# Norm weights kept in PSUM, token tiles finished in turn, channel tiles turned in two goes: the passage between the two mixers of a 1-core kernel

## What is computed

```python
# end of the first mixer
mix = jnp.concatenate([y_att, y_ssm], axis=-1)
out = jnp.einsum('bse,ed->bsd', mix, w_out[layer])
x = layer_norm(alpha * x + out, ln_g[layer], ln_b[layer])
# beginning of the second
mod = cond @ ada_w[i] + ada_b[i]
shift, scale, gate = jnp.split(mod, 3, axis=-1)
hdn = rms_norm_2(x, norm_g[i]) * (1.0 + scale[:, None, :]) + shift[:, None, :]
proj = h @ w_in          # h is hdn; w_in is 1024 x (4096 + 2048 + 32)
```

## Time and profile before

| | |
|---|---|
| median of 3 runs | 1055.65 us (1055.5 to 1058.39) |
| profiled execution | 1055.48 us, span of the trace 1053.5 us |
| PE matmul busy | 1022.1 us, 97% |
| DVE busy | 653.0 us, 62% |
| ACT busy | 434.2 us, 41% |
| POOL busy | 225.3 us, 21% |
| granted PE clock, mean | 0.997 of full speed |

### The profile page before, as it was taken

One profiled execution on the slowest core, in us unless ns is written; L12 is line 12 of the kernel. 1 busy time (PEld: TensorE's weight loads), 2 busy tenths in 40 slices (PEclk: granted clock), 3 DMA queues, 4 the chain that ended last, 5 costly groups with the idle time before them and its releaser, 6 DMA issues. The chain is left out here.

```text
span 1053.5 us, 14031 instructions
## 1 busy us (share of the span) xinstructions
PE 1022.1 (97%) x5374; PEld 830.3 (79%) x5374; DVE 653.0 (62%) x1078; ACT 434.2 (41%) x866; POOL 225.3 (21%) x169
## 2 busy tenths in 40 slices
PE   8999999999999999999899999999999998999997
PEld 5888888888766687788678788878888877888886
DVE  4254656622247778757746757785596777976726
ACT  4222333332358854332523333356423458134432
POOL 0010000000001352103100001100106873046792
PEclk9999999999999999999999999999999999999999
DMA  8277643233313242241423437435332213213502
GB/s 314 80 235 258 217 135 115 80 120 110 131 52 101 97 181 84 83 154 41 170 81 120 161 131 271 158 120 181 115 125 77 65 60 101 72 59 111 180 2 80
DMA packets 60818, 132.35 MB, mean 126 GB/s; under 512 B 6096, under 2 KB 6480, under 8 KB 60624
## 3 DMA queue, kind: packets, MB, share of 16 engines
q1 hardware_dynamic: 58304, 118.67, 33.1%
q0 software_dynamic: 2304, 12.58, 3.3%
q10 hardware_dynamic: 144, 0.20, 0.1%
HBM read 117.22 MB, written 14.22 MB: 125 GB/s over the span
## 5 line engine op out<-in xcount | busy, mean ns | idle before, releaser
L290 DVE TENSOR_TENSOR w_lo<-raw,w_hi 128x2048 fp32r<-128x2048 f32 x57 | 134.2, 2355 | 214.5 <-ACT w_hi L286 198.5
L286 ACT ACTIVATE w_hi<-raw 128x2048 fp32r<-128x2048 f32 x51 | 97.4, 1912 | 200.3 <-PE projections_ps L126 156.9
L124 PE MATMUL projections_ps<-projections_x_hi,w_hi 128*128 128x512 f32 x208 | 81.1, 390 | 0.4 <-ACTq L646 0.4
L126 PE MATMUL projections_ps<-projections_x_hi,w_lo 128*128 128x512 f32 x208 | 80.9, 389 | 0.0
L125 PE MATMUL projections_ps<-projections_x_lo,w_hi 128*128 128x512 f32 x208 | 80.9, 389 | 0.0
L124 PE MATMUL projections_ps<-w_hi,projections_x_hi 128*128 128x512 f32 x192 | 74.9, 390 | 0.0
L126 PE MATMUL projections_ps<-w_hi,projections_x_lo 128*128 128x512 f32 x192 | 74.7, 389 | 0.0
L125 PE MATMUL projections_ps<-w_lo,projections_x_hi 128*128 128x512 f32 x192 | 74.7, 389 | 0.0
L247 DVE SCALAR_TENSOR_TENSOR resid<-resid,mixer_cw 128x512 f32<-128x512 f32 x96 | 64.9, 745 | 0.0
L747 POOL TENSOR_TENSOR tok<-tok,attention_recip 128x512 f32<-128x512 f32 x8 | 8.3, 1041 | 229.9 <-DVE attention_recip L835 229.9
L124 PE MATMUL projections_ps<-w_hi,output_m_hi 128*128 128x512 f32 x128 | 51.2, 400 | 3.0 <-DVE resid L1560 1.9
(11 more groups left out here) (369 smaller groups left out, 2511.7 us busy)
## 6 DMA issues: line engine op xcount, KB each, us to landing
raw<-in_w_in SPq DMA_DIRECT2D x26, 1024.0 KB, 5.0
raw<-in_gdn_w_in SPq DMA_DIRECT2D x24, 1024.0 KB, 5.1
tok<-in_ada_w POOLq DMA_DIRECT2D x16, 768.0 KB, 6.4
raw<-in_w_out SPq DMA_DIRECT2D x8, 1024.0 KB, 5.0
qkv_kept<-mixer_ring SPq DMA_DIRECT2D x8, 1024.0 KB, 4.2
mixer_st<-qkv_kept SPq DMA_DIRECT2D x32, 256.0 KB, 2.9
raw<-in_gdn_w_out SPq DMA_DIRECT2D x7, 1024.0 KB, 5.2
resid<-in_att_bias SPq DMA_DIRECT2D x16, 256.0 KB, 2.7
```

Source lines behind the costliest of these rows:

```text
L124: nc.tensor.matmul(out, w_hi, x_hi, start=first, stop=False, skip_group_check=True)
L126: return nc.tensor.matmul(out, w_lo, x_hi, start=False, stop=last, skip_group_check=True)
L286: self.nc.scalar.activation(self.hi[s][:], self.raw[s][:], ACT.Copy).then_inc(self.hi_ready, 1)
L290: engine.tensor_tensor(self.lo[s][:], self.raw[s][:], self.hi[s][:], ALU.subtract)\
```

## The change

Five edits, all at the passage.

1. ACT copies `row_g` into two PSUM banks (`gains`), and DVE's L1625 takes its factor from there.
2. DVE finishes one token tile before it begins the next: `before_factor` and `after_factor` become one loop. POOL does `layer_factor(t)` and then `last_factor(t)`. ACT writes the scaled tile t right after its square, not after the square of the next.
3. Of the rest of the second mixer's first weight unit, DVE makes kk = 0, 1 at the end of the first block, and kk = 2, 3 in the second.
4. PE turns the token tiles 0 to 2 of the channel tiles e = 0..3 before it waits for `xn_ok`, and then token tile 3 of each.
5. In the first unit of the first block PE goes over kk outside and over e inside. The turns of the channel tiles 4 to 7 still stand ahead of each kk at e = 0. The second unit is as before.

```diff
+        early_hi, g_kept = sem("early_hi"), sem("g_kept")
+        gains = ps[:, 6:8, :].rearrange("p b c -> p (b c)")
...
@@ ACT, end of the first mixer
+                act.wait_ge(rows_in, 64)
+                act.wait_ge(added, GROUPS + TT)
+                nc.scalar.activation(gains, row_g[:], ACT.Copy).then_inc(g_kept, 1)
                 for t in range(TT):
                     if t == 2:
                         act.wait_ge(ahead[0], 48)
                         act.wait_ge(w.units_used, 9)
-                        nc.scalar.activation(w.hi[0][:], raw[0][:], ACT.Copy)
+                        nc.scalar.activation(w.hi[0][:], raw[0][:], ACT.Copy).then_inc(early_hi, 1)
...
-                    if t:
-                        act.wait_ge(factor_ok, ROW_FACTOR[t - 1])
-                        nc.scalar.activation(tok[:, t - 1, 0:D_MODEL], resid[:, t - 1, :], ACT.Copy, scale=row_f[:, t - 1:t])
+                    if t < TT - 1:
+                        act.wait_ge(factor_ok, 4 + 2 * t)
+                        nc.scalar.activation(tok[:, t, 0:D_MODEL], resid[:, t, :], ACT.Copy, scale=row_f[:, t:t + 1])
@@ POOL
-            layer_factor(0)
             for t in range(TT):
-                if t + 1 < TT:
-                    layer_factor(t + 1)
+                layer_factor(t)
                 last_factor(t)
@@ DVE, end of the first mixer
-                def before_factor(t):
+                dve.wait_ge(rows_in, 64)
+                dve.wait_ge(g_kept, 1)
+                for t in range(TT):
...
-                                                           scalar=mean_var[:, t, 0:1], in1=row_g[:],
+                                                           scalar=mean_var[:, t, 0:1], in1=gains,
                                                            op0=ALU.subtract, op1=ALU.mult))
-                    return own.n
-
-                def after_factor(t, step):
-                    dve.wait_ge(factor_ok, LAYER_FACTOR[t])
-                    own.wait(step)
+                    dve.wait_ge(factor_ok, 3 + 2 * t)
+                    own.wait()
                     nc.vector.scalar_tensor_tensor(out=resid[:, t, :], in0=resid[:, t, :], scalar=ln_f[:, t:t + 1],
                                                    in1=row_b[:], op0=ALU.mult, op1=ALU.add).then_inc(normed, 1)
-
-                dve.wait_ge(rows_in, 64)
-                step = before_factor(0)
-                for t in range(TT):
-                    next_step = before_factor(t + 1) if t + 1 < TT else None
-                    after_factor(t, step)
-                    step = next_step
                 dve.wait_ge(mod_sum, 1)
...
+                dve.wait_ge(early_hi, 1)
+                nc.vector.tensor_tensor(w.lo[0][:, 0:2, :], raw[0][:, 0:2, :], w.hi[0][:, 0:2, :], ALU.subtract)
@@ PE, beginning of the second mixer
-            def turn_x(e):
+            def turn_x(e, tiles=range(TT)):
                 if e >= 4:
                     pe.wait_ge(h_ok, e - 3)
-                for t in range(TT):
+                for t in tiles:
                     tr = nc.tensor.transpose(ps[:, 4 + e % 4, t * P:(t + 1) * P], xn[:, t, e * P:(e + 1) * P], ident)
-                tr.then_inc(h_turned, 1)
+                return tr
+            for e in range(4):
+                turn_x(e, range(TT - 1))
             pe.wait_ge(xn_ok, 1)
             for e in range(4):
-                turn_x(e)
+                turn_x(e, (TT - 1,)).then_inc(h_turned, 1)
...
+            KK_FIRST = [(kk, e) for kk in range(HALF) for e in range(4)]
+            E_FIRST = [(kk, e) for e in range(4) for kk in range(HALF)]
             pe.wait_ge(banks_free, 1)
             for s in range(2):
                 w.wait_unit(pe, s, 0)
-                for e in range(4):
-                    for kk in range(HALF):
+                for kk, e in (KK_FIRST, E_FIRST)[s]:
...
-                                turn_x(4 + kk)
+                            turn_x(4 + kk).then_inc(h_turned, 1)
@@ DVE, beginning of the second mixer
-            w.rest(nc.vector, dve, 0, 0)
+            nc.vector.tensor_tensor(w.lo[0][:, 2:HALF, :], raw[0][:, 2:HALF, :], w.hi[0][:, 2:HALF, :], ALU.subtract)\
+                .then_inc(w.lo_ready, 1)
```

More of the change, by code:

```diff
@@ L1159, in scan_and_output @@
         mod_sum = sem("mod_sum")
-        LAYER_FACTOR, ROW_FACTOR = (3, 4, 6, 8), (5, 7, 9, 10)
+        early_hi, g_kept = sem("early_hi"), sem("g_kept")
+        gains = ps[:, 6:8, :].rearrange("p b c -> p (b c)")
         def head_row(values):
@@ L1621, in before_factor @@
                     own.wait()
-                    nc.vector.bn_aggr(mean_var[:, t, :], stats[:, t, :, :].rearrange("p a b -> p (a b)"))\
-                        .then_inc(var_ok, 1)
+                    nc.vector.bn_aggr(mean_var[:, t, :], stats[:, t, :, :].rearrange("p a b -> p (a b)")).then_inc(var_ok, 1)
                     dve.wait_ge(var_ok, t + 1)
                     own.did(nc.vector.scalar_tensor_tensor(out=resid[:, t, :], in0=resid[:, t, :],
-                                                           scalar=mean_var[:, t, 0:1], in1=row_g[:],
+                                                           scalar=mean_var[:, t, 0:1], in1=gains,
                                                            op0=ALU.subtract, op1=ALU.mult))
-                    return own.n
-                def after_factor(t, step):
-                    dve.wait_ge(factor_ok, LAYER_FACTOR[t])
-                    own.wait(step)
+                    dve.wait_ge(factor_ok, 3 + 2 * t)
+                    own.wait()
                     nc.vector.scalar_tensor_tensor(out=resid[:, t, :], in0=resid[:, t, :], scalar=ln_f[:, t:t + 1],
                                                    in1=row_b[:], op0=ALU.mult, op1=ALU.add).then_inc(normed, 1)
-                dve.wait_ge(rows_in, 64)
-                step = before_factor(0)
-                for t in range(TT):
-                    next_step = before_factor(t + 1) if t + 1 < TT else None
-                    after_factor(t, step)
-                    step = next_step
                 dve.wait_ge(mod_sum, 1)
@@ L2047, in _ @@
                 w.wait_unit(pe, s, 0)
-                for e in range(4):
-                    for kk in range(HALF):
[L2050 to L2053, removed]
-                                turn_x(4 + kk)
-                            pe.wait_ge(low_ok, k + 1)
-                        mm = three_products(nc, ps[:, e, :], w.hi[s][:, kk, cols], w.lo[s][:, kk, cols],
-                                            h_hi[:, k, :], h_lo[:, k, :], k == 0, k == KT - 1)
+                for kk, e in (KK_FIRST, E_FIRST)[s]:
+                    k = HALF * s + kk
+                    cols = slice(e * P, (e + 1) * P)
+                    if e == 0:
+                        if s == 0:
+                            turn_x(4 + kk).then_inc(h_turned, 1)
+                        pe.wait_ge(low_ok, k + 1)
+                    mm = three_products(nc, ps[:, e, :], w.hi[s][:, kk, cols], w.lo[s][:, kk, cols],
+                                        h_hi[:, k, :], h_lo[:, k, :], k == 0, k == KT - 1)
                 mm.then_inc(w.units_used, 1)
```

## The result

The changed kernel takes 1059.63 us (median of 8 runs, 1057.6 to 1060.52) against 1055.81 for the kernel before: ratio 1.0033, 95% interval 1.0024 to 1.0042. It is slower, by 3.8 us. The forecast was 1056.2, and no more than 1058.2. The profiled execution took 1059.61 us, span 1057.6, 4.1 us over that of before. The repeat further down gives 1059.61 again.

What follows compares the result with a forecast made beforehand. TensorE, busy 97% of the span, was taken as the bound, its longest wait 4.6 us at the passage. Block end -0.84, first-product gain -1.17 and new wait +2.69 gave +0.68 on 1055.48: 1056.2 us, range 1053.4 to 1058.2.

Steps and rivals of the forecast that it cites:

- Channel tiles in two goes: At the passage: PE's gap 2.9 us instead of 4.64, clock stays 2.4 GHz, first product 2.01 us earlier, 1.17 from here.
- rival (b): At the passage: clock still falls, +2.6 us (1058.1), or 1059.8 if slow into the products; chance 0.14.
- a new wait of 2.7 us: At the first W_ba product: PE waits for wba_lo because the turn of e=7 comes later; +2.69 us.
- forecast +0.68: Start of the gate projection W_ba: net shift of block end (-0.84), first-product gain (-1.17) and new wait (+2.69).
- PSUM as an operand is free: L1625 at the block's end: PSUM factor costs DVE nothing and frees POOL; L1441 about 0.2 us, L1444 0.56.
- The early half holds POOL: End of first block: the early 128x1024 split delays POOL's last two steps to 504.6; block ends 0.84 us earlier, not 1.95.
- rival (c): End of first block: early split does not hold POOL, block end 1.95 us earlier, net -0.4, 1055.1; chance 0.08.
- Rival (d): Tile 3 norm: PSUM operand frees nothing, L1633 0.7 us later, total +0.1, 1056.3; shares 0.65 with the forecast.
- Tile 3's L1633: Last tile before the block's end: finishing tiles in turn starts it at 500.1 instead of 501.70, 1.6 us gained.
- Rival (a): At W_ba: PE finds wba_lo ready, so all 2.01 us stay, 1053.5, or 1052.4 if POOL gets by; chance 0.13.

Runs made afterwards that it cites:

- after_again: The changed kernel run once more without an edit: median 1059.61 us, ratio 1.0036 to the kernel before.
- one_go: The changed kernel with the fourth edit undone, PE turning all four token tiles after xn_ok: 1058.65 us, ratio 1.0019 to before.
- kk_alone: The kernel before with only the fifth edit (first unit's products by kk outside, turns ahead of each kk): 1059.24 us, ratio 1.0033 to before.
- warm_pass: The changed kernel plus eight unused PE products after the modulation sum, at the passage: 1058.35 us, ratio 1.0020 to before.
- warm_both: The changed kernel plus unused PE products both at the passage and before the W_ba wait: 1056.82 us, ratio 1.0008 to before.
- e_first: The changed kernel with the fifth edit undone, the first unit's products by e outside again: 1056.36 us, ratio 1.0004 to before.
- early_turns: The changed kernel, products still by kk outside, but all four turns of e=4..7 within kk=0: 1056.51 us, ratio 1.0002 to before.
- before_warm: The kernel before plus twelve unused PE products after the modulation sum: 1055.75 us, ratio 1.0001 to before.

## Why the prediction was wrong

**The step that failed** is in "Channel tiles in two goes": "The gap of PE is 502.34 to 505.2, 2.9 us instead of 4.64; I take it that the clock stays at 2.4 GHz." The gap came out at 3.16 and the clock fell in it, or within 0.3 us of its end, in both profiles of the changed kernel. That is rival (b), which I gave 0.14; its first product from S, 13.83, is what the trace shows (13.86). That (b) also names 1059.8 as its upper end, next to the 1059.63 measured, is luck. It reached that time by a slow clock that goes on into the first products. In both profiles of the changed kernel the clock was back at 1.00 before the first product, and the other 1.5 us came from W_ba. I took the shortening of a gap for its removal, though my own row of the kernel's end had the clock fall some 3 us after PE's last work.

**The step that was left out**: I forecast a new wait of 2.7 us and did not ask of it what I had asked of the passage. In both profiles of the changed kernel the clock falls there too (2.5 us into the wait in the first), and the W_ba products run at half speed: 1.5 us. It is not sure to fall. Of the five profiles with this wait and PE idle in it, three show the fall, in the wait or up to 1.3 us behind it (changed, after_again, one_go), and two do not (kk_alone, warm_pass). That keeping PE busy there saves the 1.5 us is shown by warm_both against warm_pass. The whole account, from S: forecast +0.68; first product 1.91 later than forecast (0.52 mis-sized, see below, and 1.39 by the clock); the chain behind it 0.27 longer; slow W_ba products 1.48. Together 4.34, the measured lag of the second unit's last product in the profiled execution. The spans differ by 4.1, the medians by 3.8.

**What held.** The wait at W_ba: 2.69 forecast, 2.65 measured, the first W_ba product 15.33 us behind the first product instead of 15.06, and the place, the releaser and the cause (kk_alone, e_first, early_turns). PSUM as an operand is free and lets POOL go: 1.28 against 1.29, and 0.19 against 1.28. The page of the Trainium skill that I had weighed, VectorE: DVE Perf Modes (section on the TRN2 errata), would have it 0.065 us dearer; the trace does not show that. The early half holds POOL: its last factor ended at 504.32, forecast 504.6 (504.34 from the same S), and the second block began at 504.90 (forecast 504.9 from the same S). So rival (c) is wrong. With both falls of the clock taken out (warm_both) the kernel is 0.8 us above before by its ratio, against 0.68 forecast.

**What was mis-sized.** At full clock the first product comes at 12.47 (e_first), not 11.95: PE begins 0.34 us behind POOL, and a transpose there costs 0.11, not 0.09, so e=0 is turned half a microsecond later. Rival (d) was wrong in its condition, for PSUM does free POOL, and too low in its price: I put 0.1 us on losing the operand. In the variant in which it was tried the second block begins 1.04 us later, and the median rises by 2.6 with the clock's share. Tile 3's L1633 waited 0.28 us for POOL, which had tile 2's row factor to do first: from S it starts 0.24 later than forecast. That cost nothing, since DVE then waited 0.75 for the modulation sum. Rival (a) did not happen: the wait stands in every profile in which the turns stand ahead of each kk.

**Left open**: what exactly decides whether the clock falls in a gap of 2 to 3 us. Across executions the slow stretches began at different points in or behind the same gap and lasted 3.4 or 6.8 us. Behind the 3.16 us gap four of five profiles show the fall; why the fifth does not, they do not show. The second edit was never undone by itself, so its own share of the time is not shown either.

## What to carry to other kernels

Before reordering a PE loop, list what stands in it that other engines wait for: here moving four groups of transposes from 1.1 us apart to 3.2 saved no wait and put the next weight unit's whole preparation on the path, while the order of the products itself was free. In this kernel a wait of PE of 2 to 3 us had two prices, its own length and, in many executions, a stretch at half clock behind it. Shortening the gap from 4.64 to 3.16 us did not take the second away. Ask for both prices of a new wait too. A single profile does not settle it: look at the mean clock of all runs. Work moved to "idle" DVE time can hold POOL if both its operands are in SBUF. Here the early half of the split did so, and the first product came 0.64 us earlier without it.

## What the runs showed of the hardware that I had not expected

- The granted clock fell after idle times of PE of 3.0 and 2.5 us in one execution, and not after 3.16 us in another of the same block (e_first), nor in the 2.65 us at W_ba in warm_pass and kk_alone. It fell in before_warm 1.4 us into a run of transposes, behind only 1.97 us of idle time; in kk_alone it stayed at 0.50 from 504.9 to 511.8 although PE was busy with transposes from 506.8.
- In early_turns the slow stretch was 6.8 us long, in the changed kernel 3.4. The eleven runs of early_turns lie up to 4.7 us apart, the slower ones at the lower mean clock.
- DVE's statistics and operations with one PSUM operand leave POOL's one-column steps at 0.19 and 0.55 us; 128x1024 operations with two SBUF operands stretch the steps that start beside them until 0.04 us behind their own end (500.11 against 500.07 before, 503.68 against 503.64 after).
